# Routing gates of an expert layer in two fp32r parts instead of three bf16 parts, with the one-hots of the first keys made on ScalarE

## The chip, the cores and the metric

The kernel runs on 1 core of one Trainium2 chip. The metric is the device time of one execution in microseconds; the kernel before takes 3236.69 us (median of 3 runs, 3233.7 to 3244.34).

## The reference, cut to what matters

Two transformer blocks over 256 tokens of width 2048. The last stage of the second is an expert layer (`peer_ffn`): 16384 experts, addressed by a pair of keys (i, j), 128 of each. Each of 8 heads picks 16 experts a token with softmax gates, 128 picks a token in all.

```python
idx = top_i[..., 0] * 128 + top_i[..., 1]        # of the 16 best pairs of each head
gates = softmax(best_s)
u = expert_down[idx];  act = gelu(einsum('tkd,td->tk', u, x))
out = einsum('tk,tkd->td', gates * act, expert_up[idx])
```

The kernel computes it densely: h[e, t] = gelu(down[e] . x[t]) for all 16384 experts, times a gate matrix G[e, t] that is zero where the token did not pick the expert, and then the product with expert_up. G of one token is a 128 x 128 matrix, the sum over the 128 picks of gate x onehot(i) x onehot(j); as a matmul it is the transposed one-hots of i (picks on the partitions) times the one-hots of j scaled by the gate.

## The kernel before, in words

**The stream.** All weights come as one stream of 1084 pieces of 128 x 1024 fp32, 512 KB each. SyncE loads a piece into `raw` (4 slots). ScalarE makes its high part (`take_hi`, L512 to L520, a copy to fp32r into `hi`, 4 slots; it waits until TensorE has used the piece four before). GpSimd makes the rest (`take_lo`, L491, `lo`, 2 slots). TensorE multiplies with `hi` and `lo`, so that the product is nearly that of fp32. Semaphores `unit_used` and `half_used` count what TensorE has used.

**The stage "peer_down"** has 128 blocks, one for each i-block of 128 experts, of 2 pieces each. `t_block` (L2022) does a block on TensorE: 16 pairs of matmuls (`pair`, L2016), one of 512 columns with the high weights (L2018) and one of 256 columns with the low ones (L2020). A block ends in one PSUM bank of four. For each block j, in this order:

- VectorE adds the block's two sums (`block_sums`, L1924, the reduce L1931) when both its pieces are used, and counts `down_summed`.
- ScalarE applies gelu (`expert_gelu`, L1005, activations L1015 and L1019) when `down_summed` has reached j + 1, and counts `free_a`.

**The order on ScalarE** is written out by hand in `gelu_rounds` (L1024). With `behind=1` a call gives, for two blocks at a time,

```python
            for half in range(2):
                for k in range(2):
                    take_hi(r + half, k)
                if not (first and 2 * half < behind):
                    expert_gelu(j0 + (2 * half - behind))
                for k in range(2, 4):
                    take_hi(r + half, k)
```

so that the gelu of block B stands behind the high parts of block B + 1 (pieces 2B + 2 and 2B + 3) and ahead of those of block B + 2 (pieces 2B + 4 and 2B + 5).

**The gates.** From block GATE0 = 48 on, TensorE makes the gate matrices between its blocks, for 4 tokens behind each of the blocks 48 to 111 (`down_blocks`, L2510, `gates_of`, L2534, the matmuls through the helper `plain`, L2112). The gate is split into three bf16 parts (L1888 to L1896), which give three matmuls of 128 columns a token, 12 a block, added up in PSUM. Their one-hots come from VectorE, into one buffer each: `one_hots` (L1900) writes `hot_i` (L1904, one instruction for 4 tokens) and `hot_j` (L1909, one a token, 3 x 128 columns) as soon as the matmuls of the group before are done (`gmat_done`), and counts `hot_done`. `gate_tokens` (L1934) then takes the gate matrices of the 4 tokens out of PSUM: for the blocks that already have their gelu it multiplies (L1941), for the others it copies the gate into `gm` (L1943); it counts `gated_done`, and TensorE writes the same bank again only two groups later. `gate_block` (L1916, L1921) multiplies the newest block's gelu with the gates that wait in `gm`.

On VectorE the order in block 48 + m is: `block_sums`, `one_hots(m + 1)`, `gate_block`, `gate_tokens(m)`.

After the gates, blocks 112 to 127 run without them, and the stage "peer_up" follows (L2555 on).

Of the kernel before, what the change touches and what calls it, by code (L numbers as in the profile page):

```python
# [21 lines left out]
F32 = mybir.dt.float32  # L22
F32R = mybir.dt.float32r
U32 = mybir.dt.uint32
BF16 = mybir.dt.bfloat16
ALU = mybir.AluOpType
ACT = mybir.ActivationFunctionType
AX = mybir.AxisListType

P = 128  # L30
# [82 lines left out]
def build(nc, stream, cols, cons, band, dil, x, rpb, w_gates, gains, p_t, w_gd, up_fb,  # L113
          qk_gain, qk_cols, sub_keys, spill, out):
    ctx = ExitStack()
    with ctx:
        def sem(name):
            return ctx.enter_context(nc.semaphore(name))
# [5 lines left out]
        def place(name, shape, at, dt=F32):  # L124
            return nc.alloc_sbuf_tensor_at(name, shape, dt, offset=base + at)
# [12 lines left out]

        i_t, j_t = (place(n, [P, T], 1024 * k) for k, n in enumerate(("i_t", "j_t")))

        gate_t = place("gate_t", [P, T, 3], 2048, BF16)
        HOTS = 4
        hot_i = place("hot_i", [P, HOTS, P], 3584, BF16)
        hot_j = place("hot_j", [P, HOTS, 3, P], 3584 + 256 * HOTS, BF16)
        assert 3584 + 1024 * HOTS <= X_AT
        RING_AT = X_AT + 32768
        W_AT = RING_AT + 40960
        assert base + W_AT + 131072 <= nc.sbuf_usable_end, (base, nc.sbuf_usable_end)
# [78 lines left out]


        hot_done, gmat_done = sem("hot_done"), sem("gmat_done")
        act_gated = sem("act_gated")  # L230
        gate_split = sem("gate_split")
        gated_done, hh_done, hl_done = sem("gated_done"), sem("hh_done"), sem("hl_done")
# [137 lines left out]
        pos_a = place("pos_a", [P, 16, 16], R_AT + 8192, U32)  # L370
        pos_b = place("pos_b", [P, 16, 16], R_AT + 9216, U32)
        route = place("route", [P, 3, 256], R_AT + 12288)
        gate_rest = place("gate_rest", [P, T], R_AT + 10240)

        top_ps = ps[:, 4, :].rearrange("p (n k) -> p n k", k=16)
        top_i = ps[:, 5, :].rearrange("p (n k) -> p n k", k=16)
# [2 lines left out]

        gm = place("gm", [P, NKEY, T], W_AT)  # L380

        GATE0 = 48
        GROUPS = T // HOTS
        iota_ps = ps[:, 7, 0:P]

        def tokens_of(m):
            return slice(HOTS * m, HOTS * m + HOTS)

        def gated_before(j):

            return HOTS * min(max(j - GATE0, 0), GROUPS)

        hg_h = place("hg_h", [P, 4, T], X_AT, F32R)
        hg_l = place("hg_l", [P, 4, T], X_AT + 4096, F32R)
# [2 lines left out]
        class Chain:  # L397
# [18 lines left out]
            def link(self, ins):  # L416
                self.inc(ins)
                self.wait()
# [84 lines left out]
        def _(act):  # L503
# [517 lines left out]

            r0 = ROUND0["peer_down"]

            def gelu_rounds(j0, r, behind=1, first=False):  # L1024

                for half in range(2):
                    for k in range(2):
                        take_hi(r + half, k)
# [4 lines that stand above are left out]
                    if not (first and 2 * half + 1 < behind):  # L1033
                        expert_gelu(j0 + (2 * half + 1 - behind))
# [9 lines left out]
            expert_gelu(GATE0 - 2)  # L1044

            act.wait_ge(routed, 1)
            for i in range(GATE0 // 4, 32):
                gelu_rounds(i * 4, i * 2 + r0)
            r0 = ROUND0["peer_up"]
# [32 lines left out]
        def _(dve):  # L1082
# [713 lines left out]
            def early_sums(*js):  # L1796
                for j in js:
                    dve.wait_ge(unit_used, after("peer_down", 2 * j + 2))
                    V.tensor_reduce(gm[:, j, :], both_sums(j % 4), AX.X, ALU.add)\
                        .then_inc(down_summed, 1)  # L1800
# [81 lines left out]
            early_sums(*range(28, 40))  # L1882
            dve.wait_ge(route_turned, 1)
            link(V.tensor_copy(iota_ps, iota))
            V.tensor_copy(i_t[:], ps[:, 4, 0:T])
            V.tensor_copy(j_t[:], ps[:, 5, 0:T])
            V.tensor_copy(gate_t[:, :, 0], ps[:, 6, 0:T]).then_inc(gate_split, 1)
            for part in range(2):  # L1888

                dve.wait_ge(gate_split, 2 * part + 1)  # L1890
                V.tensor_tensor(gate_rest[:], gate_rest[:] if part else ps[:, 6, 0:T],
                                gate_t[:, :, part], ALU.subtract).then_inc(gate_split, 1)
                dve.wait_ge(gate_split, 2 * part + 2)
                V.tensor_copy(gate_t[:, :, part + 1], gate_rest[:])\
                    .then_inc(gate_split if part == 0 else routed, 1)
                early_sums(40 + part)  # L1896
            dve.wait_ge(routed, 1)
            early_sums(*range(42, GATE0))

            def one_hots(m):  # L1900

                if m:
                    dve.wait_ge(gmat_done, m)
                chain.inc(V.tensor_tensor(  # L1904
                    hot_i[:], iota_ps.unsqueeze(1).to_broadcast([P, HOTS, P]),
                    i_t[:, tokens_of(m)].unsqueeze(2).to_broadcast([P, HOTS, P]), ALU.is_equal))
                for n in range(HOTS):
                    t = HOTS * m + n
                    ins = V.scalar_tensor_tensor(  # L1909
                        out=hot_j[:, n], in0=iota_ps.unsqueeze(1).to_broadcast([P, 3, P]),  # L1910
                        scalar=j_t[:, t:t + 1],
                        in1=gate_t[:, t, :].unsqueeze(2).to_broadcast([P, 3, P]),
                        op0=ALU.is_equal, op1=ALU.mult)
                ins.then_inc(hot_done, 1)

# [8 lines left out]
            def block_sums(j):  # L1924

                dve.wait_ge(unit_used, after("peer_down", 2 * j + 2))
                if j >= GATE0 + 2:

                    dve.wait_ge(free_a, 66 + j)
                    dve.wait_ge(act_gated, max(j - 2 - GATE0, 0))  # L1930
                V.tensor_reduce(expert_sum(j), both_sums(j % 4), AX.X, ALU.add)\  # L1931
                    .then_inc(down_summed, 1)

            def gate_tokens(m):  # L1934

                dve.wait_ge(gmat_done, m + 1)
                j = GATE0 + m + 1
                dve.wait_ge(free_a, 67 + j)
                gates = ps[:, 4 + m % 2, :].rearrange("p (t j) -> p t j", j=P)
                v = gm[:, 0:j, tokens_of(m)].rearrange("p j t -> p t j")  # L1940
                chain.inc(V.tensor_tensor(v, gates[:, :, 0:j], v, ALU.mult))  # L1941
                v = gm[:, j:NKEY, tokens_of(m)].rearrange("p j t -> p t j")
                V.tensor_copy(v, gates[:, :, j:NKEY]).then_inc(gated_done, 1)  # L1943

            def hidden_lo(p, k):

# [5 lines left out]


            one_hots(0)
            for m in range(GROUPS):
                block_sums(GATE0 + m)
                if m + 1 < GROUPS:
                    one_hots(m + 1)
                if m:
                    gate_block(GATE0 + m)  # L1960
                gate_tokens(m)
            for j in range(GATE0 + GROUPS, NKEY):
                if j == NKEY - 1:
                    hidden_lo(0, 0)
                    hidden_lo(0, 1)
                block_sums(j)
                gate_block(j)
# [36 lines left out]
        def _(pe):  # L2004
# [14 lines left out]
                         stop=False)  # L2019
                return M.matmul(t_bank(b_), w_l, xh[:, i_, :], start=False, stop=last)  # L2020

            def t_block(i, k0, bank):  # L2022


                for half in range(2):
                    k = k0 + half
                    for j in range(8):
                        if j % 4 == 0:
                            ready(i, k, j // 4)
                        kb = 8 * half + j  # L2030
                        w = [m[:, s, j * P:(j + 1) * P] for m, s in ((hi, k), (lo, k % 2))]
                        ins = pair(kb, bank, *w, kb == 0, kb == KB - 1)
                        if j == 3:
                            ins.then_inc(half_used, 1)
                        if j == 7:
                            ins.then_inc(unit_used, 1)
# [74 lines left out]
            def plain(out_ap, a, b, start, stop, **kw):  # L2111
                return M.matmul(out_ap, a, b, start=start, stop=stop, **kw)  # L2112
# [394 lines left out]

            r0 = ROUND0["peer_down"]

            def down_blocks(i, after_block=None):  # L2510
                for j in range(4):
                    pe.wait_ge(down_summed, i * 4 + (j - 3))
                    t_block(i * 2 + (r0 + j // 2), 2 * (j % 2), j)
                    if after_block:
                        after_block(i, j)

            for j in range(4):
                t_block(r0 + j // 2, 2 * (j % 2), j)
# [12 lines left out]
            with pe.Fori(10, GATE0 // 4) as i:  # L2531
                down_blocks(i)

            def gates_of(i, j):  # L2534

                m = i * 4 + (j - GATE0)
                pe.wait_ge(hot_done, m + 1)
                if not isinstance(m, int) or m >= 2:

                    pe.wait_ge(gated_done, m - 1)  # L2540
                for n in range(HOTS):
                    for part in range(3):
                        ins = plain(ps[:, 4 + j % 2, n * P:(n + 1) * P], hot_i[:, n, :],
                                    hot_j[:, n, part, :], part == 0, part == 2)
                ins.then_inc(gmat_done, 1)

            pe.wait_ge(routed, 1)
            g0 = GATE0 // 4
            down_blocks(g0, gates_of)
            with pe.Fori(g0 + 1, g0 + GROUPS // 4) as i:  # L2550
                down_blocks(i, gates_of)
            with pe.Fori(g0 + GROUPS // 4, 32) as i:
                down_blocks(i)

            def up_piece(i, k, half, first=False, last=False):  # L2555
# [151 lines left out]
```

## Time and profile before

| | |
|---|---|
| median of 3 runs | 3236.69 us |
| lowest, highest | 3233.7, 3244.34 us |
| the profiled execution: its own time | 3246.18 us |
| its span, first to last instruction | 3243.3 us |
| mean granted TensorE clock over the span | 0.997 |
| blocks 48 to 111, with the gates | 2047 to 2450 us of the span |

The profile is of one execution. Times in it are microseconds from the start of the span unless marked ns. PE is TensorE's matmuls, PEld its weight loads, DVE VectorE, ACT ScalarE, POOL GpSimd. The matmul records overlap, since matmuls are pipelined: the distance from one start to the next is what a matmul costs, not its duration. On VectorE and ScalarE too the records of neighbours overlap by some 10 to 100 ns.

### The profile page before, as it was taken

The numbers are of one execution on the slowest core, as the hardware profiler recorded it, in microseconds if no ns is written. First come the engines' busy times: TensorE is split into PE (matmuls) and PEld (weight loads), VectorE is DVE, ScalarE is ACT, GpSimd is POOL, SyncE is SP. The second block draws the span as 40 slices with busy tenths as digits, with TensorE's granted clock in tenths as the row PEclk, the third lists the DMA queues.
The fourth block names the chain that finished last, engine by engine and source line by source line (L and its number), as shares of the span: only waits on it lengthen the run. The fifth ranks groups of instructions, "written<-read, shape, count | busy, mean of one in ns | idle before, by whom it ended". The sixth has DMA issues, their size and how long they took to land.

```text
span 3243.3 us, 52110 instructions
## 1 busy us (share of the span) xinstructions
PE 3202.7 (99%) x16824; PEld 2710.8 (84%) x16824; DVE 1325.8 (41%) x2345; ACT 1504.8 (46%) x2066; POOL 2864.1 (88%) x2172
## 2 busy tenths in 40 slices
PE   9999999999999999999999999999999999999999
PEld 7777888888888888788888888888888888888887
DVE  5457244444300034556622491577773211123222
ACT  5744444334344455435443445333334555555554
POOL 6887889999899986978788889888888999999998
PEclk9999999999999999999999999999999999999999
DMA  6544555555565654554455555555455655555555
GB/s 222 170 154 159 175 179 188 184 185 187 185 204 194 198 192 136 183 164 162 145 192 186 177 185 186 175 168 165 166 168 181 213 190 192 194 192 196 192 192 180
DMA packets 160925, 588.30 MB, mean 181 GB/s; under 512 B 18080, under 2 KB 18464, under 8 KB 159808
## 3 DMA queue, kind: packets, MB, share of 16 engines
q1 hardware_dynamic: 158336, 572.59, 53.9%
q10 hardware_dynamic: 2496, 14.45, 1.2%
q8 instruction: 60, 0.98, 0.1%
q14 instruction: 33, 0.27, 0.0%
HBM read 582.78 MB, written 4.19 MB: 181 GB/s over the span
## 4 chain that ended last, share of the span: by engine, by line
PE 94%; issue 2%; DVE 2%; POOL 1%; ACT 1%; DMA 0%; SPq 0%; POOLq 0%; DVEq 0%; ACTq 0%
PE ps L2018 30%; PE ps L2020 15%; PE ps L2009 15%; PE ps L2011 15%; PE ps L2010 15%; PE ps L2112 4%; POOL lo L491 1%; DMA raw<-in_stream 0%; DVE at L1302 0%; PE ps L2107 0%; PE ps L2176 0%; DVE hx L1438 0%; PE ps L2401 0%; DVE sq_sum L1319 0%; ACT hi L520 0%
## 5 line engine op out<-in xcount | busy, mean ns | idle before, releaser
L491 POOL TENSOR_TENSOR lo<-raw,hi 128x512 fp32r<-128x512 f32 x2168 | 2863.9, 1337 | 369.4 <-PE ps L2020 133.5
L520 ACT ACTIVATE hi<-raw 128x1024 fp32r<-128x1024 f32 x1084 | 1135.9, 1058 | 1023.2 <-PE ps L2020 421.4
L2018 PE MATMUL ps<-xx,hi 128*128 128x512 f32 x4288 | 1522.1, 399 | 5.3 <-POOL lo L491 4.2
L2020 PE MATMUL ps<-xx,lo 128*128 128x256 f32 x4288 | 1202.1, 280 | 0.0
L2018 PEld LDWEIGHTS ps<-xx,hi 128*128 128x128 f32 x4288 | 805.7, 188 | 194.4 <-POOL lo L491 4.4
L2020 PEld LDWEIGHTS ps<-xx,lo 128*128 128x128 f32 x4288 | 810.8, 189 | 0.6
L2011 PE MATMUL ps<-hi,hg_l 128*128 128x512 f32 x1024 | 399.2, 390 | 0.0
L2010 PE MATMUL ps<-lo,hg_h 128*128 128x512 f32 x1024 | 398.9, 390 | 0.0
L2009 PE MATMUL ps<-hi,hg_h 128*128 128x512 f32 x1024 | 398.9, 390 | 0.0
L2009 PE MATMUL ps<-hi,xx 128*128 128x512 f32 x608 | 243.4, 400 | 7.1 <-POOL lo L491 6.9
L2011 PE MATMUL ps<-hi,xx 128*128 128x512 f32 x608 | 237.6, 391 | 0.0
L2010 PE MATMUL ps<-lo,xx 128*128 128x512 f32 x608 | 237.5, 391 | 0.0
L2009 PEld LDWEIGHTS ps<-hi,hg_h 128*128 128x128 f32 x1024 | 192.2, 188 | 45.2 <-issue 0.5
L2011 PEld LDWEIGHTS ps<-hi,hg_l 128*128 128x128 f32 x1024 | 192.3, 188 | 40.2
L2010 PEld LDWEIGHTS ps<-lo,hg_h 128*128 128x128 f32 x1024 | 192.2, 188 | 37.5
L1978 DVE TENSOR_TENSOR hg_l<-gm,hg_h 128x256 fp32r<-128x256 f32 x128 | 96.6, 755 | 249.4 <-ACT hg_h L1056 249.4
L1056 ACT ACTIVATE hg_h<-gm 128x256 fp32r (+1 forms) x256 | 106.6, 417 | 163.0 <-PE ps L2011 158.3
L1950 DVE TENSOR_TENSOR hg_l<-gm,hg_h 128x256 fp32r<-128x256 f32 x128 | 61.3, 482 | 281.4 <-ACT hg_h L1056 281.3
L1015 ACT ACTIVATE ps<-ps 128x256 f32<-128x256 f32 (+32 forms) x79 | 22.4, 283 | 300.0 <-DVE ps L1931 300.0
L2009 PEld LDWEIGHTS ps<-hi,xx 128*128 128x128 f32 x608 | 114.6, 188 | 37.7 <-POOL lo L491 10.4
L1909 DVE SCALAR_TENSOR_TENSOR hot_j<-ps,j_t,gate_t 128x384 bf16<-128x384 f32 x256 | 139.7, 608 | 0.0
L2009 PE MATMUL ps<-hi,hid_h 128*128 128x512 f32 x352 | 137.0, 389 | 0.0
(331 smaller groups left out, 2838.0 us busy)
## 6 DMA issues: line engine op xcount, KB each, us to landing
raw<-in_stream SPq DMA_DIRECT2D x1084, 512.0 KB, 3.3
gbc<-in_gains ACTq DMA_DIRECT2D x3, 1024.0 KB, 5.2
hx<-in_x SPq DMA_DIRECT2D x4, 512.0 KB, 8.5
wg<-in_w_gates ACTq DMA_DIRECT2D x1, 2048.0 KB, 8.4
bias<-in_rpb ACTq DMA_DIRECT2D x1, 2048.0 KB, 8.2
spill<-hx ACTq DMA_DIRECT2D x1, 2048.0 KB, 13.2
hx_end<-spill ACTq DMA_DIRECT2D x1, 2048.0 KB, 9.2
out<-hx_end SPq DMA_DIRECT2D x8, 256.0 KB, 3.7
```

The costliest lines, as they stand in the source:

```text
L491: nc.gpsimd.tensor_tensor(lo[:, k % 2, n], raw[:, k, n], hi[:, k, n].bitcast(F32), ALU.subtract)\
L520: nc.scalar.activation(hi[:, k, :], raw[:, k, :], ACT.Copy).then_inc(hi_done, 1)
L1056: nc.scalar.activation(hg_h[:, k, :], h, ACT.Copy).then_inc(hh_done, 1)
L1909: ins = V.scalar_tensor_tensor(out=hot_j[:, n], in0=iota_ps.unsqueeze(1).to_broadcast([P, 3, P]), scalar=j_t[:, t:t + 1], in1=gate_t[:, t, ...
L1950: V.tensor_tensor(hg_l[:, k, :], h, hg_h[:, k, :].bitcast(F32), ALU.subtract)\
L1978: V.tensor_tensor(hg_l[:, k, :], gm[:, bass.ds(i * 4 + (k - NKEY), 1), :].rearrange("p a t -> p (a t)"), hg_h[:, k, :].bitcast(F32), ALU.s ...
L2009: M.matmul(out_ap, a[0], b[0], start=start, stop=False)
L2010: M.matmul(out_ap, a[0], b[1], start=False, stop=False)
L2011: return M.matmul(out_ap, a[1], b[0], start=False, stop=stop)
L2018: M.matmul(ps[:, b_, :], w_h, xx[:, i_].rearrange("p a t -> p (a t)"), start=first, stop=False)
L2020: return M.matmul(t_bank(b_), w_l, xh[:, i_, :], start=False, stop=last)
L2112: return M.matmul(out_ap, a, b, start=start, stop=stop, **kw)
```

## The change

The gate is now split into two fp32r parts, side by side, so that one matmul of 256 columns a token gives both parts' products next to each other in PSUM, and VectorE adds the two. A group is 2 tokens (`HOTS = 2`, 128 groups): group 2b stands between the two pieces of block 48 + b, group 2b + 1 behind its second piece. `hot_i` is made by ScalarE, as Relu(1 - Abs(i - iota)), by `hot_rows(m)`, which stands in the order of ScalarE right behind the `take_hi` of piece m + 99 of the stage and counts `hot_i_done`; TensorE waits for it too. `hot_j` stays on VectorE, 2 x 128 columns a token. `gate_tokens` has three instructions for 2 tokens: a reduce of the parts into PSUM for the blocks that have their gelu, a reduce straight into `gm` for the others, and the multiply. The split of the gates before block 48 has two instructions where there were five.

```diff
-        gate_t = place("gate_t", [P, T, 3], 2048, BF16)
-        HOTS = 4
...
+        gate_t = place("gate_t", [P, T, 2], 2048, F32R)
+        HOTS = 2
...
         def gated_before(j):
-            return HOTS * min(max(j - GATE0, 0), GROUPS)
+            return min(2 * HOTS * max(j - GATE0, 0), T)
...
+            def hot_rows(m):
+
+                if m:
+                    act.wait_ge(gmat_done, m)
+                for n in range(HOTS):
+                    t = HOTS * m + n
+                    chain.inc(nc.scalar.activation(hot_i[:, n, :], iota_act[:], ACT.Abs,
+                                                   scale=-1.0, bias=i_t[:, t:t + 1]))
+                chain.wait()
+                nc.scalar.activation(hot_i[:], hot_i[:].bitcast(F32), ACT.Relu, scale=-1.0, bias=1.0)\
+                    .then_inc(hot_i_done, 1)
+
+            def take_and_rows(r, k):
+                take_hi(r, k)
+                m = 4 * (r - ROUND0["peer_down"]) + k - 2 * GATE0 - 3
+                if 0 < m < GROUPS:
+                    hot_rows(m)
+
             def gelu_rounds(j0, r, behind=1, first=False):
 
+                take_hi = take_and_rows if behind == 1 else take_plain
                 for half in range(2):
...
             act.wait_ge(routed, 1)
+            hot_rows(0)
             for i in range(GATE0 // 4, 32):
                 gelu_rounds(i * 4, i * 2 + r0)
...
             def one_hots(m):
 
                 if m:
                     dve.wait_ge(gmat_done, m)
-                chain.inc(V.tensor_tensor(
-                    hot_i[:], iota_ps.unsqueeze(1).to_broadcast([P, HOTS, P]),
-                    i_t[:, tokens_of(m)].unsqueeze(2).to_broadcast([P, HOTS, P]), ALU.is_equal))
                 for n in range(HOTS):
                     t = HOTS * m + n
                     ins = V.scalar_tensor_tensor(
-                        out=hot_j[:, n], in0=iota_ps.unsqueeze(1).to_broadcast([P, 3, P]),
+                        out=hot_j[:, n], in0=iota_ps.unsqueeze(1).to_broadcast([P, 2, P]),
                         scalar=j_t[:, t:t + 1],
-                        in1=gate_t[:, t, :].unsqueeze(2).to_broadcast([P, 3, P]),
+                        in1=gate_t[:, t, :].bitcast(F32).unsqueeze(2).to_broadcast([P, 2, P]),
                         op0=ALU.is_equal, op1=ALU.mult)
                 ins.then_inc(hot_done, 1)
...
                 dve.wait_ge(gmat_done, m + 1)
-                j = GATE0 + m + 1
+                j = GATE0 + m // 2 + 1
                 dve.wait_ge(free_a, 67 + j)
-                gates = ps[:, 4 + m % 2, :].rearrange("p (t j) -> p t j", j=P)
+                parts = ps[:, 4 + m % 2, :].rearrange("p (t a j) -> p t a j", t=HOTS, j=P)
+                both = parts.rearrange("p t a j -> p t j a")
+                sums = ps[:, 7, P:(1 + HOTS) * P].rearrange("p (t j) -> p t j", j=P)
+                if m:
+                    dve.wait_ge(gated_done, m)
+                chain.inc(V.tensor_reduce(sums[:, :, 0:j], both[:, :, 0:j], AX.X, ALU.add))
+                v = gm[:, j:NKEY, tokens_of(m)].rearrange("p j t -> p t j")
+                V.tensor_reduce(v, both[:, :, j:NKEY], AX.X, ALU.add)
+                chain.wait()
                 v = gm[:, 0:j, tokens_of(m)].rearrange("p j t -> p t j")
-                chain.inc(V.tensor_tensor(v, gates[:, :, 0:j], v, ALU.mult))
-                v = gm[:, j:NKEY, tokens_of(m)].rearrange("p j t -> p t j")
-                V.tensor_copy(v, gates[:, :, j:NKEY]).then_inc(gated_done, 1)
+                V.tensor_tensor(v, sums[:, :, 0:j], v, ALU.mult).then_inc(gated_done, 1)
...
             one_hots(0)
-            for m in range(GROUPS):
-                block_sums(GATE0 + m)
-                if m + 1 < GROUPS:
-                    one_hots(m + 1)
-                if m:
-                    gate_block(GATE0 + m)
-                gate_tokens(m)
+            one_hots(1)
+            for b in range(GROUPS // 2):
+                block_sums(GATE0 + b)
+                if 2 * b + 2 < GROUPS:
+                    one_hots(2 * b + 2)
+                if b:
+                    gate_block(GATE0 + b)
+                gate_tokens(2 * b)
+                if 2 * b + 3 < GROUPS:
+                    one_hots(2 * b + 3)
+                gate_tokens(2 * b + 1)
...
-            def down_blocks(i, after_block=None):
+            def down_blocks(i, gates_at=None):
                 for j in range(4):
                     pe.wait_ge(down_summed, i * 4 + (j - 3))
-                    t_block(i * 2 + (r0 + j // 2), 2 * (j % 2), j)
-                    if after_block:
-                        after_block(i, j)
+                    t_block(i * 2 + (r0 + j // 2), 2 * (j % 2), j,
+                            (lambda j=j: gates_at(i, j, 0)) if gates_at else None)
+                    if gates_at:
+                        gates_at(i, j, 1)
...
-                m = i * 4 + (j - GATE0)
+                m = i * 8 + (2 * (j - GATE0) + half)
                 pe.wait_ge(hot_done, m + 1)
+                pe.wait_ge(hot_i_done, m + 1)
                 if not isinstance(m, int) or m >= 2:
 
                     pe.wait_ge(gated_done, m - 1)
                 for n in range(HOTS):
-                    for part in range(3):
-                        ins = plain(ps[:, 4 + j % 2, n * P:(n + 1) * P], hot_i[:, n, :],
-                                    hot_j[:, n, part, :], part == 0, part == 2)
+                    ins = plain(ps[:, 4 + half, 2 * n * P:2 * (n + 1) * P], hot_i[:, n, :],
+                                hot_j[:, n].rearrange("p a j -> p (a j)"), True, True)
                 ins.then_inc(gmat_done, 1)
```

The rest of the diff moves `t_block`'s call for the group between the pieces, the loop bounds (`GROUPS // 8` for `GROUPS // 4`, which is the same 16 rounds), the addresses, a copy of the iota in SBUF for ScalarE, and the shorter split of the gates.

## Rows read from the trace of the kernel before

**Rows 1.** The page: busy time of the engines, and TensorE's granted clock in 40 slices

```profile
PE 3202.7 (99%) x16824; PEld 2710.8 (84%) x16824; DVE 1325.8 (41%) x2345; ACT 1504.8 (46%) x2066; POOL 2864.1 (88%) x2172
PEclk9999999999999999999999999999999999999999
```

**Rows 2.** The page: the chain that ended last, shares of the span by engine

```profile
PE 94%; issue 2%; DVE 2%; POOL 1%; ACT 1%; DMA 0%; SPq 0%; POOLq 0%; DVEq 0%; ACTq 0%
```

**Rows 3.** Waits, 2053 to 2447 us: waiting engine and line, us, times, longest

```profile
ACT ps L1015 <- DVE ps L1931: 245.3, 62, 4.1
DVE ps L1931 <- PE ps L2020: 89.2, 63, 2.3
```

**Rows 4.** Chain of waits, 2247 to 2255 us: start, us, what

```profile
2247.86 0.68 PE ps L2112 x12
2248.54 0.29 PE ps L2018
2248.83 0.12 PE ps L2020
2248.95 0.23 PE ps L2018
...
2254.15 0.69 PE ps L2112 x12
```

**Rows 5.** ScalarE's timeline, block 79: start, us, instruction, idle time before it

```profile
2248.63 0.26 ACT L1015 ACTIVATE ps<-ps 128x124 f32<-128x124 f32 x1 [3.96 <-DVE ps L1931]
2248.80 0.28 ACT L1019 ACTIVATE gm<-ps 128x132 f32<-128x132 f32 x1
2248.96 2.01 ACT L520 ACTIVATE hi<-raw 128x1024 fp32r<-128x1024 f32 x2
```

**Rows 6.** VectorE's timeline, blocks 79 and 111

```profile
2247.90 0.70 DVE L1931 TENSOR_REDUCE ps<-ps 128x256 f32<-128x512 f32 x1 [1.41 <-PE ps L2020]
2249.19 2.19 DVE L1909 SCALAR_TENSOR_TENSOR hot_j<-ps,j_t,gate_t 128x384 bf16<-128x384 f32 x4
2251.48 0.90 DVE L1941 TENSOR_TENSOR gm<-ps,gm 128x320 f32<-128x320 f32 x1
...
2450.83 1.23 DVE L1941 TENSOR_TENSOR gm<-ps,gm 128x448 f32<-128x448 f32 x1
2451.97 0.26 DVE L1943 COPY gm<-ps 128x64 f32<-128x64 f32 x1
```

**Rows 7.** Groups by line and form, 2053 to 2447 us: count, busy us, mean ns

```profile
L1904 DVE TENSOR_TENSOR hot_i<-ps,i_t 128x512 bf16<-128x512 f32 x63 | 43.6, 692 | 0.0
```

**Rows 8.** Groups by line and form, whole span, ScalarE and VectorE

```profile
L1056 ACT ACTIVATE hg_h<-gm 128x256 fp32r x252 | 105.3, 418 | 163.0 <-PE ps L2011 158.3
L1091 DVE SCALAR_TENSOR_TENSOR xx<-ps,cols_sb,xx 128x256 fp32r<-128x256 f32 x80 | 34.6, 478 | 77.2 <-ACT xx L532 77.1
L1019 ACT ACT_TABLE_LOAD x6 | 7.7, 1283 | 0.1
```

**Rows 9.** Stretches with a TensorE gap: length, PE busy, others, clock, DMA share, GB/s

```profile
203.60:210.00 6.40, 4.01 (x19) 3.48 (x19) 4.55 (x7) 2.04 (x5) 2.14 (x2) 1.00 0.45 165
230.90:237.00 6.10, 3.81 (x24) 3.32 (x24) 5.78 (x11) 1.12 (x3) 2.02 (x3) 1.00 0.36 132
1705.20:1711.00 5.80, 3.57 (x20) 3.06 (x20) 0.36 (x1) 4.10 (x4) 4.80 (x4) 1.00 0.48 165
318.50:324.40 5.90, 3.30 (x9) 2.62 (x9) 0.00 (x0) 3.89 (x4) 4.68 (x4) 0.71 0.64 218
1243.90:1254.00 10.10, 7.56 (x28) 6.28 (x28) 5.99 (x11) 5.34 (x12) 0.85 (x1) 0.66 0.01 4
7.20:14.00 6.80, 3.35 (x10) 2.71 (x10) 1.66 (x4) 3.57 (x6) 4.37 (x4) 0.75 1.02 393
```

**Rows 10.** TensorE's timeline behind one of these gaps, at half the clock

```profile
1250.91 0.63 PE L2018 MATMUL ps<-xx,hi 128*128 128x512 f32 x1
...
1251.56 0.63 PE L2018 MATMUL ps<-xx,hi 128*128 128x512 f32 x1
```

More of the change, by code:

```diff
@@ L139, in build @@
         i_t, j_t = (place(n, [P, T], 1024 * k) for k, n in enumerate(("i_t", "j_t")))
-        gate_t = place("gate_t", [P, T, 3], 2048, BF16)
-        HOTS = 4
-        hot_i = place("hot_i", [P, HOTS, P], 3584, BF16)
-        hot_j = place("hot_j", [P, HOTS, 3, P], 3584 + 256 * HOTS, BF16)
-        assert 3584 + 1024 * HOTS <= X_AT
+        gate_t = place("gate_t", [P, T, 2], 2048, F32R)
+        HOTS = 2
+        hot_i = place("hot_i", [P, HOTS, P], 4096, F32R)
+        hot_j = place("hot_j", [P, HOTS, 2, P], 4096 + 512 * HOTS, F32R)
+        assert 4096 + 1536 * HOTS <= X_AT
         RING_AT = X_AT + 32768
@@ L229, in build @@
         hot_done, gmat_done = sem("hot_done"), sem("gmat_done")
+        hot_i_done = sem("hot_i_done")
         act_gated = sem("act_gated")
@@ L372, in build @@
         route = place("route", [P, 3, 256], R_AT + 12288)
-        gate_rest = place("gate_rest", [P, T], R_AT + 10240)
         top_ps = ps[:, 4, :].rearrange("p (n k) -> p n k", k=16)
@@ L384, in build @@
         iota_ps = ps[:, 7, 0:P]
+        iota_act = place("iota_act", [P, P], 4096 + 1536 * HOTS)
+        assert 4096 + 1536 * HOTS + 512 <= X_AT
         def tokens_of(m):
@@ L1022, in _ @@
             r0 = ROUND0["peer_down"]
+            take_plain = take_hi
+            def hot_rows(m):
[13 more added lines that the diff above has]
+                    hot_rows(m)
             def gelu_rounds(j0, r, behind=1, first=False):
+                take_hi = take_and_rows if behind == 1 else take_plain
                 for half in range(2):
@@ L1884, in _ @@
             link(V.tensor_copy(iota_ps, iota))
+            link(V.tensor_copy(iota_act[:], iota))
             V.tensor_copy(i_t[:], ps[:, 4, 0:T])
@@ L1887, in _ @@
             V.tensor_copy(gate_t[:, :, 0], ps[:, 6, 0:T]).then_inc(gate_split, 1)
[L1888 to L1896, printed above, removed]
+            dve.wait_ge(gate_split, 1)
+            V.tensor_tensor(gate_t[:, :, 1], ps[:, 6, 0:T], gate_t[:, :, 0].bitcast(F32),
+                            ALU.subtract).then_inc(routed, 1)
             dve.wait_ge(routed, 1)
-            early_sums(*range(42, GATE0))
+            early_sums(*range(40, GATE0))
             def one_hots(m):
@@ L1954, in _ @@
             one_hots(0)
-            for m in range(GROUPS):
-                block_sums(GATE0 + m)
-                if m + 1 < GROUPS:
-                    one_hots(m + 1)
-                if m:
-                    gate_block(GATE0 + m)
-                gate_tokens(m)
-            for j in range(GATE0 + GROUPS, NKEY):
+            one_hots(1)
[9 more added lines that the diff above has]
+                gate_tokens(2 * b + 1)
+            for j in range(GATE0 + GROUPS // 2, NKEY):
                 if j == NKEY - 1:
@@ L2020, in pair, with t_block @@
                 return M.matmul(t_bank(b_), w_l, xh[:, i_, :], start=False, stop=last)
-            def t_block(i, k0, bank):
+            def t_block(i, k0, bank, between=None):
                 for half in range(2):
                     k = k0 + half
+                    if half and between:
+                        between()
                     for j in range(8):
@@ L2532, in _, with gates_of @@
                 down_blocks(i)
-            def gates_of(i, j):
-                m = i * 4 + (j - GATE0)
+            def gates_of(i, j, half):
+                m = i * 8 + (2 * (j - GATE0) + half)
                 pe.wait_ge(hot_done, m + 1)
+                pe.wait_ge(hot_i_done, m + 1)
                 if not isinstance(m, int) or m >= 2:
@@ L2549, in _ @@
             down_blocks(g0, gates_of)
-            with pe.Fori(g0 + 1, g0 + GROUPS // 4) as i:
+            with pe.Fori(g0 + 1, g0 + GROUPS // 8) as i:
                 down_blocks(i, gates_of)
-            with pe.Fori(g0 + GROUPS // 4, 32) as i:
+            with pe.Fori(g0 + GROUPS // 8, 32) as i:
                 down_blocks(i)
```

## The prediction, made before the changed kernel was built or run

> **What bounds the kernel now.** I read the page first: TensorE is busy for 99% of the span at the full clock [rows 1], and the chain that ended last is TensorE for 94% [rows 2]. What any other engine is spared is worth nothing in itself; what counts is TensorE's own work and any moment in which it waits.
>
> Then the stretch that the change touches. In blocks 48 to 111 others wait for TensorE: VectorE's sums wait for it, and ScalarE's gelu waits for those sums, 4 us a block [rows 3]. No wait of TensorE on another engine is among them. The chain shows one block: it is TensorE alone, 6.29 us from one group of 12 gate matmuls to the next (2247.86 to 2254.15). The 12 take 0.68 us; a pair of the block takes 0.12 + 0.23 = 0.35 us, 16 of them 5.55 us; the first matmul after the group is 0.06 us longer than the others [rows 4].
>
> The third view is the order of the neighbours in that same block. The block's last matmul gives way at 2247.86; VectorE's sum starts at 2247.90 [rows 6]; ScalarE's gelu starts at 2248.63, in two pieces, and only behind it, from 2248.96, come the two high parts, 2.01 us together [rows 5]. So ScalarE's high parts for block B + 2 stand behind the gelu of block B, and thus behind the end of block B on TensorE. They are about a block and a half early today, and nobody notices.
>
> **The change, part by part.** All of it acts in 64 blocks.
>
> *TensorE's matmuls.* Out go 12 matmuls, 0.68 us. In come 4 of 256 columns in fp32r. The pair's second matmul has that shape and its own weights, 0.12 us [rows 4]; 4 take 0.47. There are two breaks in a block instead of one, so 0.06 us more. Net: 0.68 + 0.06 - 0.47 - 0.12 = 0.15 us less a block, 10 us in all. It lies on the path.
>
> *VectorE's work.* `hot_i` leaves, 0.69 us a block [rows 7]. `hot_j` shrinks from 384 to 256 columns: 4 took 2.19 us [rows 6], and for 256 columns the nearest row of the same operation is 0.48 us [rows 8], so 4 take at most 1.9. `gate_tokens` grows. Its multiply took 0.90 us for 320 elements and 1.23 for 448 [rows 6], 2.6 ns each; half as many elements, but twice a block, is 0.49 and 0.65 us each time. The two reduces of a group read 512 elements together; a reduce of 512 takes 0.70, and the short copy shows that a second instruction costs at most 0.26 [rows 6]: about 0.9. So a group's tokens take 1.4 to 1.55 us. Sum with sums and gate block (0.70, at most 0.4): 5.2 to 6.1 us a block, against some 6.1 of TensorE if it never waited. That would be tight; the next part gives it 3 us more of room.
>
> *ScalarE's new work and where it stands.* This decides. By the index in `take_and_rows`, `hot_rows(m)` comes behind the high part of piece m + 99. With m = 2b + 1 that is piece 2b + 100 = 2(48 + b) + 4, the first piece of block B + 2 where B = 48 + b. In `gelu_rounds` that high part stands behind the gelu of block B. The gelu waits for the sums of B, and those for the last matmul of B. But TensorE wants the one-hots of group 2b + 1 immediately behind that last matmul. So in each of the 64 blocks TensorE stops there until this chain has run:
>
> - last matmul to VectorE's sum: 0.04 us (2247.86 to 2247.90); sum to gelu: 0.73 (to 2248.63) [rows 5, 6]
> - gelu in two pieces: 0.33 (to 2248.96); one high part: half of 2.01, 1.00 [rows 5]
> - two Abs of 128 columns: by the gelu of 124 columns 0.17 until the next may start, then 0.28 for the second to end [rows 5]; a wait on ScalarE's own semaphore, taken like that between engines, 0.04; Relu of 256 columns: the nearest row is the copy of 256, 0.42 [rows 8]. Together 0.91
> - signal to TensorE, and the weight load ahead of its first matmul: not shown by a row of this kind; at least 0.04, and up to 0.3. I take 0.1.
>
> Sum: 0.04 + 0.73 + 0.33 + 1.00 + 0.91 + 0.1 = 3.1 us. From below it is 2.7 (if the small activations overlap fully), from above 3.4. The other group of the block, 2b + 2, doesn't wait: its one-hots follow one high part and one `hot_rows` later, 1.9 us, and TensorE has 8 pairs, 2.8 us, to do first. VectorE is queued behind the same stop: `one_hots(2b + 2)` waits for the matmuls of 2b + 1. From there to the end of `gate_tokens(2b)`, for which group 2b + 2 waits, it needs 0.05 + 0.9 + 0.4 + 1.55 = 2.9 us in the last blocks and under 2.8 in the others; that costs 2 us in all at most. GpSimd and the DMA queue get more time for each piece than today, so nothing new comes from them; the later high parts still are more than one block early. Stop and saving together: 3.1 - 0.15 = 2.95 us a block, **189 us**.
>
> *The clock behind each stop.* TensorE has six gaps of 2.2 to 3.5 us in this trace. In the rows each gap is the length less the busy time [rows 9]. Behind three (2.4, 2.3, 2.2 us) the clock stayed whole, and in three stretches (2.6, 2.5 and 3.45 us idle, the 2.5 in two gaps of 2.3 and 0.2) its mean is 0.71, 0.66 and 0.75. Half of the clock missing for 2 x 0.29 x 5.90 = 3.4 us, 6.9 and 3.4 us. So it goes to the 1.2 GHz level after about half of such gaps, the longest two included. At that level a pair takes 0.65 us (1250.91 to 1251.56) instead of 0.35 [rows 10]: 3.4 us at half clock lose 3.4 x (1 - 0.35/0.65) = 1.55 us. Gaps of 3.1 us are nearer to those that fell; I take 0.7 falls a stop, 1.05 us, **67 us** in 64. The ends are none (0) and each (99).
>
> The Trainium skill, TensorE: Matmul & The Clock Gate, in "HAM oscillation — how this bites in real kernels", tells of a loop whose wait in each round puts the clock back each time, so that the price is paid in every round. By that it would be 99 us where I take 67; half of the gaps of this trace agree.
>
> *The table of ScalarE.* No table load is on a gelu that alternates with copies in this stage: 6 loads of 1283 ns stand on L1019 in the whole span [rows 8]. That Abs and Relu share the table no row shows. The Trainium skill, ScalarE: Activation LUTs, in "Table sets: the hidden batching unit", says that cheap functions such as relu, copy and abs are in every set. I put loads at zero; the rival below has their price.
>
> *Ahead of the gates.* The shorter split of the gates and the first `hot_rows` run beside blocks 40 to 47, where VectorE and ScalarE wait for TensorE: nothing.
>
> **The sum.** 189 + 67 = 256 us. The profiled execution took 3246.2 us, so 3502; it stands 9.5 above the median of the three runs, which gives 3236.7 + 256 = 3493.
>
> **The rivals.**
>
> - *The stop, with the clock whole.* For it: three of six gaps left it whole. Against it: these stops are longer than those. 189 us, 3426.
> - *The stop, and a fall at each.* For it: the two longest gaps fell, and a stop comes back every 9 us. 189 + 99 = 288, 3525.
> - *ScalarE loads a table for Abs and again for gelu.* Both loads lie on the chain of the stop: 2 x 1.28 x 64 = 164, with a fall at each stop: 288 + 164 = 452, 3689. Against it: the page named above.
> - *The one-hots come in time, so that only the saving is left (the other side).* It would need `hot_rows(2b + 1)` to be done when TensorE ends block 48 + b, that is at least 3.1 us earlier than the order of `gelu_rounds` allows. Then 10 us are saved, 3227. The point from which it decides is a stop under 0.15 us. Against it: the order is fixed in the code, and ScalarE's wait for the sums of the same block is in the trace [rows 3].
> - *Same, VectorE late:* the one-hots in time, but `gate_tokens(2b)` late by 0.1 to 0.2 us a block, which gives back the 10 us: 3237.
>
> **The numbers.** Forecast 0.65, clock whole 0.12, a fall at each stop 0.15, table loads 0.03, in time 0.04, in time but VectorE late 0.01. The range takes in the first three with the bounds of the chain: low, 2.7 - 0.15 = 2.55 us in 64 blocks, 163 us, 3400; high, 3.4 - 0.15 + 1.55 = 4.8 us, 307 us, 3544, and a little for a fall that lasts longer: 3555. About 0.3% is what a measurement of this kernel can tell from no change (its three runs spread by that). Faster by more: 0.04; within: 0.01; slower by more: 0.95.
>
> **What would show it.** In the profile after: a new wait of TensorE, weight loads or matmuls of L2112's successor on ScalarE's Relu, 64 times, about 3 us each, some 190 us; the chain that ended last running in these blocks through the sum, the gelu, the high part, Abs and Relu; a block taking 9 to 11 us; TensorE's busy share down to about 92 to 94% of a longer span; the granted clock between 0.7 and 0.9 there, 1.00 elsewhere; ScalarE's gelu still waiting for the sums; all other stages as before. The forecast is wrong if TensorE's waits there are under 1 us a block, if the clock stays at 1.00 (then near 3426), if table loads appear, or if VectorE's `gate_tokens` is what TensorE waits for.

## The result, and the profile after

The changed kernel takes 3579.45 us (median of 6 runs, 3577.9 to 3589.21) against 3236.52 us of the kernel before beside it: 1.1057 times as long, 95% interval 1.104 to 1.1074, or 343 us more. The forecast was 3493 us with a range up to 3555. The direction and the mechanism came out, the size was too small.

The page of the changed kernel: span, busy time, clock, DMA, the chain that ended last, and its new matmuls [against rows 1, 2].

```profile
span 3587.4 us, 51880 instructions
PE 3334.1 (93%) x16312; PEld 2807.4 (78%) x16312; DVE 1296.3 (36%) x2535; ACT 1628.6 (45%) x2450; POOL 2858.5 (80%) x2172
...
PEclk9999999999999999999999978777877999999999
DMA  6545455555555545445555522222222465555555
...
PE 88%; issue 6%; DVE 2%; ACT 2%; POOL 1%; DMA 0%; SPq 0%; POOLq 0%; DVEq 0%; ACTq 0%
...
L2142 PE MATMUL ps<-hot_j,hot_i 128*128 128x256 f32 x256 | 71.2, 368 | 212.1 <-issue 157.6
```

TensorE is no longer at 99%. The eight slices with a clock of 7 or 8 and a DMA of 2 are blocks 48 to 111, and 212.1 us of idleness stand in front of the gate matmuls alone. The rest of the kernel is as it was: the span without the stretch from the first gate matmul to the last is 2846 us before and after (3243.3 - 397.4 and 3587.4 - 741.7). Who is waited for, in that stretch (waits of TensorE, 2048 to 2790 us: us, times, longest):

```profile
PE ps L2142 <- issue: 157.6, 48, 3.3
PE ps L2142 <- ACT hot_i L1039: 54.5, 16, 3.4
```

These are 64 stops, one a block, of 3.3 us. The view puts only 16 of them down to the Relu (L1039) and gives "issue", a wait for nothing that it can see, for the other 48. Here the order of time helps, since all stops look alike. The chain of waits, that is the work followed back from each start to what released it, through one that was attributed (2236.87 to 2249.20 us; start, us, what):

```profile
2236.87 0.13 PE ps L2048
2237.00 0.02 issue
2237.03 0.71 DVE ps L1949
2237.74 0.02 issue
2237.76 0.02 ACT ps L1019
2237.78 0.10 issue
2237.88 0.33 ACT gm L1023
2238.21 0.94 ACT hi L524
2239.15 0.59 ACT hot_i L1036 x2
2239.73 0.02 issue
2239.76 0.42 ACT hot_i L1039
2240.18 0.23 issue
2240.41 0.79 PE ps L2142 x2
2241.20 0.43 PE ps L2046
2241.62 0.21 PE ps L2048
...
2246.16 0.23 PE ps L2142 x2
...
2249.20 3.28 issue
```

That is the chain of the forecast, link by link: sum, gelu, one high part, Abs, Relu, and only then TensorE [rows 4 to 6 are the same places before]. 3.41 us lie between 2237.00 and 2240.41. The stop shown is one of 15 longer ones: there 0.23 us pass between the end of the Relu and the first gate matmul, in the 49 others 0.10 to 0.14, so that most stops leave TensorE idle for 3.28 us (212.1 / 64 = 3.31 in the mean). Behind it a pair takes 0.43 + 0.21 = 0.64 us instead of 0.35: TensorE is at its 1.2 GHz level. At 2246.16 the two gate matmuls between the pieces take 0.23 us; they wait for nothing. The stretches of the clock (length, busy PE, PEld, DVE, ACT, POOL, clock, DMA share, GB/s):

```profile
2240.40:2246.00 5.60, 5.59 (x19) 4.86 (x20) 2.01 (x6) 1.83 (x4) 1.27 (x1) 0.51 0.12 47
2246.00:2249.20 3.20, 3.20 (x20) 2.56 (x18) 1.89 (x5) 0.00 (x0) 2.54 (x2) 1.00 0.16 27
...
2048.00:2790.00 742.00, 529.23 (x2291) 445.34 (x2290) 306.41 (x763) 279.79 (x637) 327.64 (x257) 0.79 0.27 92
```

Over the 742 us the mean is 0.79, so 2 x 0.21 x 742 = 312 us were at half. A fall is here one stretch at the 1.2 GHz level. Counted in the trace there are 64, one for each stop; 37 lasted 3.4 us and 27 lasted 6.8, 311 us in all.

ScalarE's work by form in that stretch, with its table loads of the whole span on the gelu; ScalarE's timeline in the stop shown above; and VectorE's timeline of one group:

```profile
L524 ACT ACTIVATE hi<-raw 128x1024 fp32r<-128x1024 f32 x129 | 135.3, 1049 | 0.0
L1036 ACT ACTIVATE hot_i<-iota_act,i_t 128x128 fp32r<-128x128 f32 x254 | 87.4, 395 | 1.2
L1039 ACT ACTIVATE hot_i<-hot_i 128x256 fp32r<-128x256 f32 x127 | 52.9, 416 | 4.0
...
L1023 ACT ACT_TABLE_LOAD x6 | 7.7, 1283 | 0.1
```

```profile
2238.09 1.06 ACT L524 ACTIVATE hi<-raw 128x1024 fp32r<-128x1024 f32 x1
2239.03 0.69 ACT L1036 ACTIVATE hot_i<-iota_act,i_t 128x128 fp32r<-128x128 f32 x2
2239.76 0.42 ACT L1039 ACTIVATE hot_i<-hot_i 128x256 fp32r<-128x256 f32 x1
```

```profile
2234.21 0.88 DVE L1927 SCALAR_TENSOR_TENSOR hot_j<-ps,j_t,gate_t 128x256 fp32r<-128x256 f32 x2 [2.24 <-PE ps L2142]
2235.00 0.42 DVE L1962 TENSOR_REDUCE ps<-ps 128x128 f32<-128x256 f32 x1
2235.33 0.42 DVE L1964 TENSOR_REDUCE gm<-ps 128x128 f32<-128x256 f32 x1
2235.66 0.43 DVE L1967 TENSOR_TENSOR gm<-ps,gm 128x128 f32<-128x128 f32 x1
```

No table load stands on the Abs or the Relu, none on anything in this stretch, and the gelu has 6 in the whole span as before. VectorE is quicker than I took it for: a group's tokens take 1.1 us at this block (2235.00 to 2236.09) and 1.3 in the last ones (2783.73 to 2785.05), where I had 1.4 to 1.55.

### The profile page after: what moved, and what is told of

It is laid out like the page before. It is cut to its first block, busy times and chain, and to the rows that moved or that the text cites. A ratio compares the mean times of both kernels' runs of the same rounds, so it can differ in the third digit from the quotient of the medians.

```text
span 3587.4 us, 51880 instructions
## 1 busy us (share of the span) xinstructions
PE 3334.1 (93%) x16312; PEld 2807.4 (78%) x16312; DVE 1296.3 (36%) x2535; ACT 1628.6 (45%) x2450; POOL 2858.5 (80%) x2172
## 4 chain that ended last, share of the span: by engine, by line
PE 88%; issue 6%; DVE 2%; ACT 2%; POOL 1%; DMA 0%; SPq 0%; POOLq 0%; DVEq 0%; ACTq 0%
PE ps L2046 29%; PE ps L2048 14%; PE ps L2037 13%; PE ps L2039 13%; PE ps L2038 13%; PE ps L2142 4%; POOL lo L495 1%; ACT hi L524 1%; DMA raw<-in_stream 0%; DVE at L1328 0%; DVE ps L1949 0%; PE ps L2137 0%; PE ps L2206 0%; ACT hot_i L1036 0%; ACT hot_i L1039 0%
## 5 line engine op out<-in xcount | busy, mean ns | idle before, releaser
L2046 PE MATMUL ps<-xx,hi 128*128 128x512 f32 x4288 | 1633.9, 421 | 6.7 <-POOL lo L495 4.2
L2048 PE MATMUL ps<-xx,lo 128*128 128x256 f32 x4288 | 1252.8, 292 | 0.0
L2046 PEld LDWEIGHTS ps<-xx,hi 128*128 128x128 f32 x4288 | 864.4, 202 | 218.3 <-POOL lo L495 4.5
L2048 PEld LDWEIGHTS ps<-xx,lo 128*128 128x128 f32 x4288 | 866.6, 202 | 0.6
L2142 PE MATMUL ps<-hot_j,hot_i 128*128 128x256 f32 x256 | 71.2, 368 | 212.1 <-issue 157.6
L1927 DVE SCALAR_TENSOR_TENSOR hot_j<-ps,j_t,gate_t 128x256 fp32r<-128x256 f32 x256 | 112.2, 480 | 380.3 <-PE ps L2142 380.3
L2142 PEld LDWEIGHTS ps<-hot_j,hot_i 128*128 128x128 f32 x256 | 51.0, 246 | 235.1 <-issue 230.9
L1974 DVE TENSOR_TENSOR hg_l<-gm,hg_h 128x256 fp32r<-128x256 f32 x128 | 82.5, 647 | 260.3 <-ACT hg_h L1082 260.2
L2006 DVE TENSOR_TENSOR hg_l<-gm,hg_h 128x256 fp32r<-128x256 f32 x128 | 54.4, 425 | 291.5 <-ACT hg_h L1082 291.5
```

The source lines that it names most:

```text
L1927: ins = V.scalar_tensor_tensor(out=hot_j[:, n], in0=iota_ps.unsqueeze(1).to_broadcast([P, 2, P]), scalar=j_t[:, t:t + 1], in1=gate_t[:, t, ...
L1974: V.tensor_tensor(hg_l[:, k, :], h, hg_h[:, k, :].bitcast(F32), ALU.subtract)\
L2006: V.tensor_tensor(hg_l[:, k, :], gm[:, bass.ds(i * 4 + (k - NKEY), 1), :].rearrange("p a t -> p (a t)"), hg_h[:, k, :].bitcast(F32), ALU.s ...
L2046: M.matmul(ps[:, b_, :], w_h, xx[:, i_].rearrange("p a t -> p (a t)"), start=first, stop=False)
```

## The experiments

All runs are edits of the changed kernel and compute the same; e2, e7 and e8 add matmuls of no use. Ratios are to the kernel before, run beside them, whose median there was 3245 to 3246 us (3236.52 beside the changed kernel); so kernels of different rows are compared by their ratios. The table gives the stretch from the first to the last gate matmul, 63.5 blocks, as the traces have it; the block before is the one of [rows 4]. "Idle" is how long the matmuls of the gates waited there; "falls, us at half" counts the falls of the clock and adds their time, as far as it lies in the stretch.

| kernel | us | ratio, interval | stretch, us | a block, us | idle, us | falls, us at half |
|---|---|---|---|---|---|---|
| before | 3245 | 1 | | 6.29 | 0 | 0 |
| changed | 3579 | 1.1057, 1.104 to 1.1074 | 741.7 | 11.68 | 212 | 64, 305 |
| e1 rows earlier | 3268.28 | 1.0074, 1.0057 to 1.0091 | 420.7 | 6.63 | 18 | 0 |
| e2 stop filled, 22 | 3458.62 | 1.0659, 1.0639 to 1.0678 | 615.6 | 9.69 | 38 | 0 |
| e3 rows ahead of hi | 3496.11 | 1.0776, 1.0758 to 1.0794 | 650.7 | 10.25 | 152 | 63, 212 |
| e4 rows on VectorE | 3259.16 | 1.0049, 1.0028 to 1.0069 | 414.9 | 6.53 | 10 | 0 |
| e5 rows in time | 3240.56 | 0.9988, 0.9976 to 1.0 | 396.5 | 6.24 | 1 | 0 |
| e6 and gate_block later | 3234.01 | 0.9969, 0.9957 to 0.9981 | 389.0 | 6.13 | 0 | 0 |
| e7 stop filled, 12 | 3496.26 | 1.077, one run | 651.1 | 10.25 | 115 | 24, 79 |
| e8 stop filled, 16 | 3460.63 | 1.066, one run | 616.1 | 9.70 | 84 | 0 |

**e1: is it the order alone?**

```diff
-                m = 4 * (r - ROUND0["peer_down"]) + k - 2 * GATE0 - 3
+                m = 4 * (r - ROUND0["peer_down"]) + k - 2 * GATE0 - 2
```

> Edit: the changed kernel with hot_rows(m) one high part earlier in ScalarE's order (behind piece m + 98 instead of m + 99), so that the rows of group 2b + 1 stand ahead of the gelu of block 48 + b and no longer wait for that block's sums. Theory (the order alone makes the stops, and the stops make the clock fall): no wait of TensorE on the Relu, clock 1.00, a block of the gates takes 6.1 to 6.2 us, in all 3225 to 3240 us, some 350 us less than the changed kernel. Rival 1 (the 128-column group between two pieces, or VectorE's longer taking-out, holds TensorE): waits on VectorE of 0.3 us and more a block, over 3250 us. Rival 2 (the half clock comes from the new mix of matmuls and not from the stops): clock still near 0.8 in these blocks and over 3350 us.

Measured: 1.0074, no half clock at all. One digit in an index takes the ratio from 1.1057 to 1.0074, that is 318 of the 343 us. Rival 2 falls: the same mix of matmuls runs at the whole clock. Of rival 1 the time came (over 3250 us), but not the waits on VectorE of 0.3 us a block: only 8.2 us of weight loads in all, 11 times, are put down to it. The time lies outside what I expected, by some 20 us if the ratio is taken, and most of it is another wait. The waits of TensorE in e1, 2049 to 2471 us:

```profile
PE ps L2142 <- ACT hot_i L1039: 14.0, 45, 0.5
PE ps L2142 <- issue: 4.3, 18, 0.2
```

Now the other group of each block waits: its rows stand behind a high part that starts after the gelu. The chain in e1 (start, us, what):

```profile
2254.05 0.59 ACT hot_i L1036 x2
2254.64 0.02 issue
2254.66 0.42 ACT hot_i L1039
2255.08 0.09 issue
2255.18 0.47 PE ps L2142 x2
```

After such a wait the two gate matmuls take 0.47 us of the chain instead of 0.23, so each short wait costs another 0.25 us for starting anew. With 18 / 64 = 0.28 us of idleness that makes the 0.50 us by which a block of e1 is longer than one of e6 (6.63 and 6.13), the run below in which nothing waits.

**e2: what is the stop, and what the clock behind it?**

```diff
                 pe.wait_ge(hot_done, m + 1)
-                pe.wait_ge(hot_i_done, m + 1)
                 if not isinstance(m, int) or m >= 2:
 
                     pe.wait_ge(gated_done, m - 1)
+                if half:
+                    for _ in range(22):
+                        plain(ps[:, 5, 0:T], xh[:, 0, 0:P], xh[:, 0, :], True, True)
+                pe.wait_ge(hot_i_done, m + 1)
```

> Edit: the changed kernel, order unchanged, but TensorE does 22 extra matmuls of 256 columns (of no use, 0.12 us each, 2.6 us) ahead of its wait for the rows of group 2b + 1, into the bank that the group overwrites next. They fit into the stop of 3.4 us, so the stop stays as long and only the idleness in it goes. Theory (a fall of the clock follows the idle stop, and costs some 125 us of the 343): clock 1.00 throughout, a block takes 9.5 to 9.6 us from sum to sum, in all 3440 to 3465 us, though the 64 stops still last 3.4 us each. Rival (the clock falls for another reason, or the stop itself is longer than the chain of rows says): clock under 0.9 and 3550 us or more.

Measured: 3458.62 us, inside the range, and in e2's stretch the clock is whole:

```profile
2044.00:2660.00 616.00, 576.31 (x3701) 514.81 (x3699) 307.23 (x762) 277.11 (x638) 331.44 (x257) 1.00 0.33 110
```

So the two shares can be read off the table. A block takes 11.68 us with the stop empty and 9.69 with it filled: (11.68 - 9.69) x 64 = 127 us are the clock. Against e6, which has no stop, 9.69 - 6.13 = 3.56 us, x 64 = 228 us, are the stop. The filling left the stop's length alone: from the start of the block's last low matmul to that of the gate matmul it is 3.52 us in e2 and 3.56 in the changed kernel (median of 64), so at most 0.04 x 64 = 3 us of the 127 are something else. The falls can also be priced one by one in the traces. From the first gate matmul behind the stop to the block's last low matmul TensorE takes 6.14 us in e2; in the changed kernel it takes 7.59 us in the 37 blocks with a fall of 3.4 us and 8.74 in the 26 complete ones with a fall of 6.8. That is 1.45 and 2.60 us a fall, and 37 x 1.45 + 27 x 2.60 = 124 us.

**e3: the stop made shorter by one link**

```diff
             def take_and_rows(r, k):
-                take_hi(r, k)
                 m = 4 * (r - ROUND0["peer_down"]) + k - 2 * GATE0 - 3
                 if 0 < m < GROUPS:
                     hot_rows(m)
+                take_hi(r, k)
```

> Edit: the changed kernel with hot_rows(m) ahead of the high part of piece m + 99 instead of behind it, so that the stop's chain loses one high part (0.94 us in the chain of waits) and keeps the sum, the gelu, Abs and Relu. Theory: the stop is 2.5 us instead of 3.4. That alone gives back 60 us. What the clock does behind stops of 2.5 us is open between two readings: if each stop still brings a fall as 3.4 us did, some 110 to 125 us stay and the time is near 3510 us; if only about half do (in the trace of before gaps of 2.2 to 2.6 us fell in two of five), some 60 us stay, and the time is 3440 to 3460 us. Rival (the high part does not lie on the chain): stop 3.4 us, time as the changed kernel, near 3580 us.

Measured: 3496.11 us. The high part is a link, for the stop's idleness is 2.34 us now (the chain in e3):

```profile
2258.78 2.34 issue
2261.12 0.77 PE ps L2142 x2
```

And of the two readings of the clock the first is right: 63 of 64 stops of 2.3 us brought a fall, all of 3.4 us, though gaps of 2.2 to 2.4 us in the kernel before mostly did not [rows 9]: of four such gaps one brought a fall. A check on the price: the block would take 6.13 + 3.56 - 0.94 = 8.75 us at the whole clock, and takes 10.25; 1.50 x 64 = 96 us, that is 1.52 us for each of 63 falls.

**e4: the new parts alone, with VectorE making both one-hots.** ScalarE's rows and TensorE's wait for them are taken out, and

```diff
                     dve.wait_ge(gmat_done, m)
+                chain.inc(V.tensor_tensor(
+                    hot_i[:], iota_ps.unsqueeze(1).to_broadcast([P, HOTS, P]),
+                    i_t[:, tokens_of(m)].unsqueeze(2).to_broadcast([P, HOTS, P]), ALU.is_equal))
```

> Edit: the changed kernel with the one-hots of the first keys left to VectorE (one comparison of 256 columns a group, as before the change but for 2 tokens), nothing new on ScalarE: the two side-by-side parts alone. Theory (the parts and their taking-out are nearly free, the move to ScalarE makes all of the loss): no wait on ScalarE; VectorE needs about 5.5 us of 6.15 a block, and its tokens of group 2b are late by 0.1 to 0.5 us for the group two later, so a block takes 6.15 to 6.6 us, in all 3230 to 3260 us, clock 1.00. Rival (the layout in two groups a block costs by itself): over 3300 us.

Measured: 3259.16 us, at the upper end of what was expected. The loss of 343 us is that of the move to ScalarE, in its place in the order; the two parts side by side cost nothing like it. VectorE is then too late by itself; its waits in e4's stretch, 2053 to 2470 us:

```profile
PEld ps L2144 <- issue: 24.3, 48, 0.8
PE ps L2144 <- DVE gm L1969: 9.5, 30, 0.5
```

L1969 is the last instruction of `gate_tokens`: TensorE waits for the bank to be taken out. So there is a reason to take work from VectorE.

**e5: all rows in time**

```diff
             def take_and_rows(r, k):
-                take_hi(r, k)
-                m = 4 * (r - ROUND0["peer_down"]) + k - 2 * GATE0 - 3
+                m = 4 * (r - ROUND0["peer_down"]) + k - 2 * GATE0 - 2
+                if m % 2:
+                    take_hi(r, k)
                 if 0 < m < GROUPS:
                     hot_rows(m)
+                if m % 2 == 0:
+                    take_hi(r, k)
```

> Edit: the run with the rows one high part earlier, and besides the rows of an even group (the one between the two pieces) ahead of their high part, those of an odd group still behind it. In that run TensorE still waited for the even groups' Relu, 0.3 to 0.5 us of idleness and some 0.25 us for starting anew, and lost some 20 us. Theory (that wait is all that is left): rows 1 us earlier than wanted, no wait on the Relu; VectorE's taking-out of the even group ends 2.9 us after the end of the block, just in time until late, with waits of up to 0.3 us in the last 15 blocks; in all 3232 to 3240 us against 3236.5 to 3245 before, that is 0.995 to 1.000 of it. Rival (two fp32r matmul groups a block cost more than the 12 bf16 ones): 1.003 and more with no wait in the trace.

Measured: 0.9988, the interval ends at 1.0: the loss is gone, a gain is not told from none. No wait on the Relu is left; those that are, 2053 to 2450 us in e5, grow towards the end of the stretch (none in its first 100 us, up to 0.5 us at its end) and are VectorE's, those called "issue" too, for e6 removes them by a move on VectorE alone:

```profile
PEld ps L2145 <- issue: 8.7, 28, 0.5
PEld ps L2145 <- DVE gm L1970: 1.5, 7, 0.3
```

**e6: and VectorE's gate_block behind the even group's tokens**

```diff
-                if b:
-                    gate_block(GATE0 + b)
                 gate_tokens(2 * b)
+                if b:
+                    gate_block(GATE0 + b)
```

> Edit: the run with both rows in time, and VectorE's gate_block behind gate_tokens(2b) instead of ahead of it, which ends the tokens that TensorE's next even group waits for 0.1 to 0.4 us earlier. Theory: no wait on VectorE is left even in the last blocks; up to 5 us less than that run, 0.993 to 0.998 of the time before. Rival (something else is late by then): the same time as without the move.

Measured: 0.9969 (0.9957 to 0.9981), 10 us less than before. This is the change with its ordering repaired. It beats the changed kernel clearly and the kernel before by 0.3%, which is small, but the interval leaves out 1. Its waits of TensorE in the same stretch, and then a row of the whole stretch, 2048 to 2450 us:

```profile
PEld ps L2145 <- issue: 0.3, 2, 0.2
```

```profile
2048.00:2450.00 402.00, 402.00 (x2363) 352.64 (x2362) 305.57 (x770) 281.83 (x642) 333.32 (x265) 1.00 0.51 173
```

**e7 and e8: how much of the stop must be filled.** As e2, with `range(12)` and `range(16)`.

> Edit: the changed kernel with the stop filled in part, 12 useless matmuls instead of 22. The stop keeps its 3.4 us, TensorE idles about 1.8 us of it. If the clock falls after any stop of this size, half clock and near 3550 us; if 1.8 us in 9.6 are too short to bring it down, the clock stays at 1.00 and the time is that of the filled stop, 3450 to 3460 us.

> Edit: the same with 16 useless matmuls, TensorE idles about 1.3 us of the stop. Expected: clock 1.00, 3450 to 3460 us; a clock under 0.99 would say that even such short stops bring it down.

Measured, one run each:

```profile
2048.00:2699.00 651.00, 534.55 (x3058) 466.69 (x3056) 306.91 (x762) 276.30 (x637) 330.66 (x257) 0.94 0.31 104
```

```profile
2049.00:2666.00 617.00, 531.17 (x3319) 469.13 (x3317) 307.37 (x762) 277.45 (x638) 331.81 (x257) 1.00 0.33 110
```

The first is e7. It did neither of the two things I had offered: with 1.8 us idle in each stop the clock fell at 24 of 64, and a block took 10.25 - 9.69 = 0.56 us more than in e2, 36 us in all or 1.5 us for each fall. The second, e8, with 1.3 us, fell at none and gave the time of the filled stop, as expected.

## Why the prediction was right and wrong

*What bounds the kernel, and where the stop comes from:* right. From the index and from the place of the gelu in ScalarE's order it followed that the rows of group 2b + 1 come a whole chain late, and e1 shows that this one place makes the loss.

*The saving on TensorE, 0.15 us a block, 10 us:* right. e6 has 6.13 us a block against 6.29, 0.16 x 64 = 10 us, and runs at 0.9969. Its costs on VectorE were rather too high, and hidden by the stop, as I said; only e1, e4 and e5 show that VectorE and the even groups come next. I had written that the even group doesn't wait: that held only beside the stop.

*The stop, 3.1 us:* 0.46 us too short. It is 3.56 us by e2 and e6; 228 us, less 10, instead of the 189 us I summed. Two terms were mis-sized. From the first Abs to the Relu 0.73 us pass (2239.03 to 2239.76), where I had 0.45 + 0.04 from gelus of 124 and 132 columns without a pointer as bias; an Abs takes 395 ns. The high part gives back 0.06 of that (2238.09 to 2239.03, for 1.00). And for the signal and the start I took 0.1 us, with 0.3 at most: the signal is 0.10 us in most stops and 0.23 in some, but the first matmuls behind the wait cost 0.25 more. My upper bound of 3.4 us left out that TensorE starts anew.

*The clock, 67 us, with ends 0 and 99:* this is the step that failed. It is 127 us, outside my own bounds, and with the longer stop it puts a block at 11.68 us where I had 9 to 11. The price of a fall of 3.4 us was right (1.55 us taken; 1.52 by e3, 1.45 by the blocks of the changed kernel). The number was wrong: I took 0.7 falls a stop, from three in six gaps of the trace, and it is 64 in 64. And the length was wrong: I put every fall at 3.4 us, while a row in front of me showed one of 6.9 us [rows 9]. 64 falls at 1.55 us are 99 us; nearly all of the other 28 comes from the 27 that lasted 6.8, at 2.60 us each. The upper bound should have priced the long fall. (0.7 of 1.55 us is 1.09, not the 1.05 I wrote, which is 2 us in the sum.)

*The sum:* 228 - 10 + 127 = 345 us, 343 measured. The likeliest case should have been the rival with a fall at each stop (3525 us), and that too would have been 55 us short. The rule of the Trainium skill that the price is paid in each round (TensorE: Matmul & The Clock Gate, "HAM oscillation — how this bites in real kernels") held here, 64 stops and 64 falls; my sum went by the gaps of the trace before, of which half fell.

*The table loads:* none, as the Trainium skill has it (ScalarE: Activation LUTs, "Table sets: the hidden batching unit"): no load stands on L1036 or L1039 in the trace after, and the gelu has no more of them than before.

*The rival on the other side:* it needed the rows in time. e5 and e6 made that kernel; 10 us were foretold for it, and e6 is 10 us faster. Its neighbour, the same with VectorE late, is e5: a block takes 6.24 us instead of 6.13, and 7 of the 10 us are gone.

What stays open: how the chip decides on a fall. In the changed kernel 24 of the 27 falls of 6.8 us began 0.67 to 1.39 us before TensorE started again, and 3 began 0.4 us before, where shorter ones lie too; every later one lasted 3.4 us. That is an observation, and no run varied it alone.

## What to carry to other kernels

When work moves to an engine with slack, write down what stands in front of it in that engine's order, up to what that itself waits for: 46% busy says nothing if the new work stands behind a wait for the very event that it has to precede. Here one position in an index was worth 318 us. A stop of 2.3 us and more that comes back every round costs its length and, here, over half as much again in clock (127 on 228 us); price each return of it, and the longest fall that the trace shows.

## What the runs showed of the hardware that I had not expected

- Stops of TensorE that come back once a block: 1.3 us idle brought down the clock at 0 of 64, 1.8 us at 24 of 64, 2.34 us at 63 of 64, 3.28 us at 64 of 64. Filling 1.9 us of the stop with 16 matmuls of no use (e8) took the ratio from 1.106 to 1.066, so that the kernel was nearly 130 us faster than the changed one. The figures of 1.3 and 1.8 us rest on one run each.
- The falls of the changed kernel lasted 3.4 us (37) or 6.8 us (27), and cost 1.45 and 2.60 us each.
- Behind a wait the first two matmuls of 256 columns take 0.47 us of the chain instead of 0.23 at the whole clock: a wait costs some 0.25 us beyond its idleness.
- An Abs of 128 columns from SBUF with a bias from a pointer takes 395 ns, a gelu of 124 to 132 columns from PSUM with none 260 to 280 ns [rows 5], while Relu of 256 columns takes 416.
